# A hybrid diffusion block on one core: first token loads ahead of the first border, inverse transforms in the order of their inputs, VectorE combines in wider operations, precision splits after the third border

## The reference, cut to what matters

```python
def long_conv(u, kf, bias):
    length = u.shape[1]
    uf = jnp.fft.rfft(u, n=2 * length, axis=1)
    y = jnp.fft.irfft(uf * kf[None], n=2 * length, axis=1)[:, :length]
    return y + u * bias.astype(jnp.float32)

def hyena_branch(z, rows, conv_w, conv_b, filt, hy_bias):
    length = z.shape[1]
    z = short_conv_rows(z, rows, conv_w, conv_b).astype(jnp.float32)
    v, x1, x2 = jnp.split(z, 3, axis=-1)
    kf = hyena_filter_spectra(length, *filt)
    y = x1 * long_conv(v, kf[:, 0], hy_bias[0])
    return x2 * long_conv(y, kf[:, 1], hy_bias[1])
...
        hc = modulate(rmsnorm(ctx, norm1_g[l]), csh1, csc1)
...
        h = modulate(rmsnorm(x, norm1_g[l]), sh1, sc1)
        z = h @ w_in[l]
        u = z[..., HY_COLS:].astype(jnp.float32)
        st_f, st_b = s5_states(u, *s5_par, init_f, init_b)
        y = jnp.concatenate([hyena_branch(z[..., :HY_COLS], rows, conv_w[l], conv_b[l], filt, hy_bias[l]),
                             s5_readout(u, st_f, st_b, *s5_out)], axis=-1)
        x = x + g1[:, None] * (y.astype(x.dtype) @ w_out[l])
```

## Time and profile before

| what | value |
|---|---|
| timed runs, median (lowest to highest) | 2510.84 us (2508.46 to 2514.4), 3 runs |
| profiled execution, its own time | 2506.11 us |
| its span | 2504.4 us |
| `prepare` to the first border | about 239 us |
| `mix` | 239.5 to 534 us |
| `long_convs` | 535 to 751 us |
| TensorE, VectorE, ScalarE, GpSimd busy | 93%, 77%, 53%, 14% of the span |

### The profile page before, as it was taken

How to read it: one execution, slowest core, us unless ns; L and a number is a source line. 1 busy time by engine, 2 the same in 40 slices (tenths; PEclk the granted TensorE clock), 3 DMA queues, 4 the chain that set the end, 5 groups by cost and what they waited for, 6 DMA issues and landing times.

```text
span 2504.4 us, 27973 instructions
## 1 busy us (share of the span) xinstructions
PE 2330.7 (93%) x10978; PEld 1775.9 (71%) x10978; DVE 1940.8 (77%) x1424; ACT 1317.3 (53%) x788; POOL 361.7 (14%) x190
## 2 busy tenths in 40 slices
PE   7887989999988947999999999999999999999997
PEld 2334877853445835888888888888888888888886
DVE  4765799837584467888888888888888888888887
ACT  2123422210023216777777677677677677677766
POOL 0543400000002000012012022022022021021011
PEclk9898999999999967999999999999999999999998
DMA  7657344454432255999999999999999999999997
GB/s 271 226 226 261 123 110 128 138 213 149 151 147 85 85 235 185 379 376 366 374 378 373 366 378 374 372 372 379 370 370 377 374 369 375 379 367 373 378 360 294
DMA packets 199344, 726.40 MB, mean 290 GB/s; under 512 B 14050, under 2 KB 60034, under 8 KB 180277
## 3 DMA queue, kind: packets, MB, share of 16 engines
q1 hardware_dynamic: 190878, 694.03, 73.5%
q0 software_dynamic: 5328, 21.50, 3.1%
q10 hardware_dynamic: 3080, 10.09, 1.1%
HBM read 678.40 MB, written 47.17 MB: 290 GB/s over the span
## 4 chain that ended last, share of the span: by engine, by line
PE 55%; DVE 3%; issue 3%; ACT 1%; DMA 0%; POOL 0%; DVEq 0%; ACTq 0%; PEldq 0%; POOLq 0%
PE psum L2143 14%; PE psum L2130 13%; PE psum L2131 13%; PE psum L2132 13%; DVE w_low L2226 3%; PE psum L2111 2%; ACT x_high L2166 1%; ACT w_high L2162 0%; DVE arena L2240 0%; DMA out<-arena 0%; DVE x_low L2230 0%; DVE arena L2286 0%; DVE arena L2282 0%; POOL out L2091 0%; DVEq L2280 0%
## 5 line engine op out<-in xcount | busy, mean ns | idle before, releaser
L2226 DVE TENSOR_TENSOR w_low<-w_raw,w_high 128x4096 fp32r<-128x4096 f32 (+2 forms) x288 | 1164.1, 4065 | 95.3 <-ACT w_high L2162 95.3
L2162 ACT ACTIVATE w_high<-w_raw 128x4096 fp32r<-128x4096 f32 (+2 forms) x288 | 964.1, 3348 | 467.2 <-PE psum L2132 260.5
L2130 PE MATMUL psum<-w_high,x_high 128*128 128x512 f32 (+1 forms) x1536 | 578.0, 376 | 20.0 <-DVE w_low L2226 17.5
L2131 PE MATMUL psum<-w_low,x_high 128*128 128x512 f32 (+1 forms) x1536 | 573.5, 373 | 0.0
L2132 PE MATMUL psum<-w_high,x_low 128*128 128x512 f32 (+1 forms) x1536 | 571.9, 372 | 0.0
L2130 PEld LDWEIGHTS psum<-w_high,x_high 128*128 128x128 f32 x1536 | 290.0, 189 | 80.9 <-DVE w_low L2226 25.1
L2132 PEld LDWEIGHTS psum<-w_high,x_low 128*128 128x128 f32 x1536 | 289.2, 188 | 52.1
L2131 PEld LDWEIGHTS psum<-w_low,x_high 128*128 128x128 f32 x1536 | 289.7, 189 | 49.7
L2143 PE MATMUL psum<-w_high,a_high 128*128 128x512 f32 x704 | 220.8, 395 | 0.0
L2078 POOL TENSOR_TENSOR arena<-arena 1x1 f32<-1x1 f32 x15 | 63.2, 4214 | 1089.1 <-DVE arena L2282 1089.1
L2143 PE MATMUL psum<-w_low,a_high 128*128 128x512 f32 x704 | 217.3, 390 | 0.0
(11 more groups left out here) (361 smaller groups left out, 2638.9 us busy)
## 6 DMA issues: line engine op xcount, KB each, us to landing
w_raw<-in_ex_w_down SPq DMA_DIRECT2D x80, 2048.0 KB, 9.3
w_raw<-in_ex_w_gate SPq DMA_DIRECT2D x64, 2048.0 KB, 9.9
w_raw<-in_ex_w_up SPq DMA_DIRECT2D x64, 2048.0 KB, 10.5
w_raw<-in_ex_w_gate SPq DMA_DIRECT2D x32, 1536.0 KB, 10.4
w_raw<-in_ex_w_up SPq DMA_DIRECT2D x32, 1536.0 KB, 7.3
arena<-in_mod_w SPq DMA_DIRECT2D x24, 1024.0 KB, 6.2
w_raw<-in_ex_w_down SPq DMA_DIRECT2D x16, 1024.0 KB, 8.2
scratch_spec<-arena SPq DMA_DIRECT2D x8, 1024.0 KB, 10.2
```

The lines of the kernel that those rows point to most:

```text
L2130: nc.tensor.matmul(o, xt_h[:, x], h[:, f], start=kk == 0, stop=False)
L2131: nc.tensor.matmul(o, xt_h[:, x], l[:, f], start=False, stop=False)
L2162: nc.scalar.activation(high[n % NHI][:, 0:w], raw[n % NS][:, 0:w], ACT.Copy).then_inc(hi_done, 1)
L2226: nc.vector.tensor_tensor(low[n % NS][:, 0:w], raw[n % NS][:, 0:w], high[n % NHI][:, 0:w].bitcast(F32), ALU.subtract).then_inc(lo_done, 1)
```

## The change

Four edits, in words:

1. **First border.** The loads of the first 5 token tiles and of the first weight chunk are issued by SP in `prepare`, after the last filter matrices and before the last two writes of spectra. Their slots lie in memory that `prepare` no longer uses, and `c_high` and `c_low` move to where the slots were. The waits for the writes go from the end of `prepare` into `mix`: ACT waits for the S5 tables ahead of its first `high_tile` and for the spectra ahead of `scaled(4)`; SP waits for the S5 tables where it reads them. POOL's wait stays.
2. **Inverse transforms.** All eight banks take output tiles. The order is kk 0 of tiles 0 to 3, kk 1 of tiles 0 to 3, kk 0 and 1 of tiles 4 to 7, and then kk 2 of all eight.
3. **Combines.** The same arithmetic in 8 operations of 1024 or 2048 elements a partition (12 where f is 1).
4. **Splits.** The row blocks' high parts (4 on ACT) and the low parts (3 and 4 on VectorE) move into `output_and_route`; TensorE waits for them after the 32 matmuls of the S5 gate. The 3 high parts of weights stay.

```diff
@@ prepare, SyncE
             dft(7)
+            sp.wait_ge(used, NU)
+            for n, xin_slot in enumerate(k.token_slots):
+                src = k.i["x"][0, (n - 2) * P:(n - 1) * P, :] if n >= 2 else k.i["ctx"][0, n * P:(n + 1) * P, :]
+                sp.dma_start(xin_slot, src).then_inc(k.tokens_got[n], 16)
+            c = FIRST_CHUNK
+            sp.dma_start(k.w_in_first, k.i["w_in"].rearrange("l (k p) n -> p (l k) n", p=P)[:, :, c * P:(c + 1) * P]).then_inc(k.first_weights, 16)
             spec_out(2)
             spec_out(3)
-            for s in range(2):
-                sp.wait_ge(sput[s], 64)
             sp.wait_ge(rowput, 128)
@@ prepare, ScalarE
             quarter(3)
-            act.wait_ge(put_in, 64)
-            act.wait_ge(put_lw, 64)
@@ mix, SyncE
-            tokens(0)
-            tokens(1)
-            weights(0)
-            tokens(2)
-            tokens(3)
             weights(1)
-            tokens(4)
             weights(2)
-            for n in range(5, NT):
+            for n in range(NX, NT):
                 tokens(n)
+            sp.wait_ge(k.tables_in, 64)
             in_tables(0)
@@ mix, ScalarE
             high_part(0)
+            act.wait_ge(k.tables_in, 64)
+            act.wait_ge(k.local_put, 64)
             high_tile(0)
             high_tile(1)
+            for s in range(2):
+                act.wait_ge(k.spec_put[s], 64)
             scaled(4)
@@ long_convs, TensorE
                 pe.wait_ge(read, 4 * order + 3)
-                pe.wait_ge(done, 4 * order + 2 + order)
+                pe.wait_ge(done, 4 * order + 2)
                 for n in range(4):
-                    backward(order, n, (order,))
+                    backward(order, n, (0,))
                 pe.wait_ge(done, 4 * order + 3)
                 for n in range(4):
-                    backward(order, n, (1 - order,))
-                pe.wait_ge(done, 4 * order + 4)
-                for n in range(4):
-                    backward(order, n, (2,)).then_inc(inv, 1)
+                    backward(order, n, (1,))
                 pe.wait_ge(ring[2], loads + 32)
                 pe.wait_ge(ring[3], loads + 32)
+                pe.wait_ge(read, 4 * order + 4)
                 for n in range(4, 8):
-                    pe.wait_ge(fin, 8 * order + n - 3)
-                    backward(order, n, (order, 1 - order, 2)).then_inc(inv, 1)
+                    backward(order, n, (0, 1))
+                pe.wait_ge(done, 4 * order + 4)
+                for n in range(8):
+                    backward(order, n, (2,)).then_inc(inv, 1)
@@ long_convs, VectorE, combine (the 12 operations with the spectrum become these 4)
+                tt(bars(y), bars(x), kre, ALU.mult)
+                link(tt(bars(x), bars(x), kim, ALU.mult))
+                tt(y[:, 0:4:3, :], y[:, 0:4:3, :], x[:, 1:3, :], ALU.add)
+                link(tt(y[:, 1:3, :], y[:, 1:3, :], x[:, 0:4:3, :], ALU.subtract))
@@ output_and_route, TensorE, after the S5 gate
             pe.wait_ge(wlo, 1)
+            pe.wait_ge(wlo_first, 3)
+            pe.wait_ge(xlo, 4)
```

More of the change, by code:

```diff
@@ L240, in prepare @@
     dgot = [k.sem(f"d_got{s}") for s in range(2)]
-    sput = [k.sem(f"d_put{s}") for s in range(2)]
     row_banks = (6, 0)
@@ L1514, in backward @@
                 par, tile = divmod(n, 4)
-                o = ps[:, bank(order, 0) + n % 4, :]
+                o = ps[:, bank(par) + tile, :]
                 e, h = divmod(tile, 2)
-                first = order
                 for kk in kks:
```

131 lines of the change are left out of this document (56 added, 75 removed).

## The result

| | before | changed |
|---|---|---|
| median of the timed runs | 2510.43 us (2508.46 to 2514.4, 4 runs) | 2477.09 us (2473.23 to 2477.85, 4 runs) |
| profiled execution, its span | 2506.11, 2504.4 | 2477.30, 2475.5 |

The ratio is 0.9862, with a 95% interval from 0.9845 to 0.9879. The forecast was 2481.3 for the median and 2476.6 for the profiled execution.

The account below looks back on a forecast made before the run. TensorE, busy 93%, was taken as the bound, with its standstills in the first 752 us as the target. Terms 8.8 + 8.7 + 9.8 + 2.2 = 29.5 us, so 2510.8 - 29.5 = 2481.3 us; range 2475 to 2489.

Parts of the forecast that it names:

- First border, 8.8 us: Start of `mix`: ACT scales the first tile 8.8 us earlier, and VectorE, which paces the front, passes all on.
- Rival E: Little changes: a wait deeper in `mix` meets the border's gain and one order keeps its wait; 2500 us, chance 0.05.
- What hides the moved waits: In `mix`: tables land 4 us before ACT needs them, spectra are waited for 2 us later still; no cost charged.
- rival A: First border: moved loads delay squares, POOL's table, the last table or `mix`'s tiles; 2 to 6 us, 2483 to 2487, chance 0.18.
- Inverse transforms, 8.7 and 9.8 us: Long convolutions: TensorE never waits inside an inverse, each takes 41.3 us; 8.7 us saved in the first order, 9.8 in the second.
- the tightest spot: Second forward of f 0: ring slot 0's reload lands at 632.2, TensorE wants it at 633.0; 0.8 us to spare.
- rival C: Ring slot 0's reload comes too late, TensorE waits 9 us and the clock falls again; 2493 us, chance 0.04.
- Combines, nothing on the path: Long convolutions: wide combines save VectorE 5 us an order, but TensorE has its results early already; worth nothing, only slack.
- rival D: Combines: wide operations with steps between runs go at the rate of scattered elements; 31 us slower, 2542, chance 0.03.
- Splits and third border, 2.2 us: Third border: one `gated` follows the last matmul instead of 3.5 us of splits; 2.2 us gained, moved splits cost nothing.
- The clock at the third border, taken as 0 with 2.2 at the other end: S5 gate's start: clock assumed to fall in the shorter pause too, so gain 0; 2.2 us if it does not.
- rival B: Clock stays up at the third border and comes back sooner in `mix`'s front; 2.2 us more, 2479, chance 0.10.

Follow-up runs that it names:

- early split: Changed kernel with the first weight chunk's high and low parts also made at the end of the first stage; 2475.25 us, ratio 0.9863.
- combines undone: Changed kernel with the combines back in operations of 512, the rest kept; 2480.07 us, ratio 0.9877.
- order alone: Kernel before with only the new order of the inverse transforms and the eight banks it needs; 2499.7 us, ratio 0.9955.
- combines alone: Kernel before with only the combines in operations of 1024 and 2048; 2501.13 us, ratio 0.997.
- splits alone: Kernel before with only the splits moved into the next stage; 2506.28 us, ratio 0.9982.
- waits and loads: Changed kernel with the waits back at the first stage's end, 2484.71 us; and, separately, with the six loads issued by `mix` again, 2483.17 us.

## Why it came out so, step by step

**First border, 8.8 us: right at the place it was read, 0.6 to 1.8 less by the end of `mix`.** The front went from 10.40 to 1.59 us, 8.8 exactly. The prediction went on that VectorE, which paces the front of `mix`, would pass all of it on. It passed on 7.0 in this pair of profiles. Over the five profiles with the edit and nothing more at the border, `mix` takes 293.8 to 295.0 us, over the six without any of it 302.1 to 303.7 (means 294.6 and 302.8), 8.2. The step that was off is "VectorE too, since it had no idle time in which a part could get lost": its instructions can get longer. The low part of the first weights took 1.22 us before, and the second one 2.94:

```profile
251.76 1.22 DVE L1299 TENSOR_TENSOR p_wlow<-p_wraw,p_whigh 128x1024 fp32r<-128x1024 f32 x1
...
258.00 2.94 DVE L1299 TENSOR_TENSOR p_wlow<-p_wraw,p_whigh 128x1024 fp32r<-128x1024 f32 x1
```

In the changed kernel they took 3.01 and 2.16 us:

```profile
244.00 3.01 DVE L1309 TENSOR_TENSOR p_wlow<-p_wraw,p_whigh 128x1024 fp32r<-128x1024 f32 x1
...
252.04 2.16 DVE L1309 TENSOR_TENSOR p_wlow<-p_wraw,p_whigh 128x1024 fp32r<-128x1024 f32 x1
```

So 1.8 us are lost at the first and 0.8 won back at the second, 1.0 in all. The distance from ScalarE's first scaling to VectorE's first copy of 128x512 says the same: 42.89 us before (243.44 to 286.33), 43.91 now (235.68 to 279.59); it is 42.9 in five of the six profiles without the edit and 43.7 to 44.0 in the five with it. The other 0.8 of this pair lies behind that copy, in a stretch that takes 247.6 to 250.5 us over the fourteen profiles; it is of the size of their scatter. For the first of the two operations GpSimd has a subtraction of its own, at 243.57, beside VectorE's of 244.00:

```profile
243.57 2.36 POOL L1287 TENSOR_TENSOR p_clow<-p_h,p_chigh 128x1024 fp32r<-128x1024 f32 x1 [19.54 <-ACT p_chigh L1182]
```

In the six profiles in which GpSimd's came first, by 0.2 to 0.6 us, VectorE's took 2.84 to 3.23 us; in the seven in which it came 0.5 to 1.0 us behind, VectorE's took 1.21 to 1.23. That GpSimd's work is the cause was not tested by itself; the early split takes this operation out of `mix`, and its `mix` is 1.5 us shorter. Rival E, a wait deeper in `mix`, did not come.

**What hides the moved waits: right, and rival A's collisions cost nothing on the path.** Neither the tables nor the spectra were waited for in `mix`. The queue's length did show, where the prediction had looked: GpSimd's last table took 9.9 us to land, by the view of DMA issues from 200 to 240 us of the changed kernel, instead of the 4.2 of the earlier trace rows, and GpSimd came to the border at 233.4 instead of 226.6, still 1.1 us ahead of ScalarE's 234.5. ScalarE's loads for the means took 7.4 us in the median of four (6.1 before), and two squares waited for them, 2.27 and 0.91 us. The mean was not later for it: from VectorE's 128x10 operation to the issue of `s_local` are 4.09 us in both profiles. The transfers:

```profile
scratch_s_out<-arena POOLq DMA_DIRECT2D x1, 1024.0 KB, 9.9
...
arena<-in_x ACTq DMA_DIRECT2D x4, 512.0 KB, 7.4
```

By the Trainium skill ("DMA: Bandwidth & Descriptors", "Queues, rings and completion order") a DMA engine takes turns between the queues that have work, a packet at a time. By that rule a queue beside a full one becomes slower and doesn't stand behind it. The rows agree, the 9.9 us as well: from 215 to 230 us, around that write, the windows give the DMA engines a busy share of 0.56 before and 1.03 now. The prediction's reading, that it costs nil, holds for a moment at which the queue was full already; at GpSimd's write it had not been.

**Inverse transforms, 8.7 and 9.8 us: right, 8.8 and 9.6 measured.** Forward to inverse to forward, TensorE's timeline of the changed kernel:

```profile
529.10 57.37 PE L1520 MATMUL psum<-arena 128*128 128x512 f32 x128 [1.62 <-PEq L181]
586.31 41.36 PE L1534 MATMUL psum<-arena 128*128 128x512 f32 x96
627.51 55.10 PE L1520 MATMUL psum<-arena 128*128 128x512 f32 x128
682.44 7.07 PE L1538 MATMUL psum<-arena 128*128 128x256 f32 x32
```

The first inverse took 41.2 us, the second 41.45 (682.44 to 723.89), at a clock of 1.00. The saving was 8.8 and 9.6. The reload of ring slot 0, "the tightest spot", came in time (rival C out).

**Combines, nothing on the path: right for the inverses in this order, and only there.** With the new order, plain combines leave the convolutions at 194.7 and 195.7 us against 194.8. But a term was missing behind them: with the new order and combines of 512 the norm row comes too late at the third border, and in combines undone the pause is 0.7 us longer and the gate 1.7. With the old order the same edit is worth 9.5 (203.3 against 212.8). So the 18.5 us are not the order's alone: the order alone brings 18.1, the combines alone 9.5, both together 18.0, because they cure one wait. Read from the changed kernel, undoing the order costs 9.8 us, half of what the prediction's terms say, and that is no contradiction. On VectorE they cost what was forecast: 11.70 us for a plain one (578.98 to 590.68) and 18.76 for f 1 (forecast 11.7 and 18.7), and no operation pays for its strides or its repeated operand (rival D out):

```profile
551.02 2.28 DVE L1612 TENSOR_TENSOR arena<-arena 128x2048 f32<-128x2048 f32 x1
553.34 1.23 DVE L1613 TENSOR_TENSOR arena<-arena 128x1024 f32<-128x1024 f32 x1
554.49 1.22 DVE L1614 TENSOR_TENSOR arena<-arena 128x1024 f32<-128x1024 f32 x1
...
578.98 1.22 DVE L1605 TENSOR_TENSOR arena<-psum,arena 128x1024 f32<-128x1024 f32 x1
...
590.68 1.22 DVE L1605 TENSOR_TENSOR arena<-psum,arena 128x1024 f32<-128x1024 f32 x1
```

An order needs 56 instructions fewer. VectorE saved 4.9 us (58.72 to 53.86), 0.09 us for each; by the 157 ns of the Trainium skill ("VectorE: DVE Perf Modes", "The TRN2 errata") it would be 8.8. The spacing of the rows was the right price.

**Splits and third border, 2.2 us: the sum right, the share wrong.** The pause went from 4.40 to 2.01 us, and no split was waited for at the gate's end:

```profile
725.90 5.69 DVE L1827 TENSOR_TENSOR g_wlow<-arena,g_whigh 128x1024 fp32r<-128x1024 f32 x3 [0.86 <-PEq L181]
731.51 4.62 DVE L1830 TENSOR_TENSOR g_xlow<-arena,g_xhigh 128x1024 fp32r<-128x1024 f32 x4
```

But the prediction set the moved splits against the border of before, and never asked what the new order does to that border. It lengthens the pause by 4.3 to 5.9 us when the splits stay (8.69 and 10.34). With the new order, the splits' edit is worth 6.7 us of pause, and 2.9 more at the gate; without it, 2.4 and 0.5.

**The clock at the third border, taken as 0 with 2.2 at the other end: the other end came.** The gate took 27.70 us instead of 29.92, at a granted clock of 1.00 from its start. This is rival B's gain at this border. It belongs to no single edit: without the wide combines the gate took 29.40 us although the splits were moved (splits alone, combines undone). The profiled executions then add up: 7.0 in mix, 18.0 in the convolutions (8.8 and 9.6, and 0.2 in the second forward, less 0.6 in the first, where the clock fell at another place), 2.4 and 2.2 make 29.7; less 1.05 by which the first stage came out longer, and with 0.3 behind the gate, it is the 28.9 us between the spans.

**The step from profile to median: what is left open.** The medians differ by 33.3 us, the profiled executions by 28.8. The kernel before was profiled in an execution faster than all four timed ones of the result; the changed kernel's profile fell on its median. Over the 14 profiles `s_local` is issued from 230.9 to 243.4 us. That does not go with the border's edit (mean 236.4 with the loads in the first stage and 237.7 without) but with TensorE's granted clock in the first stage. Its mean from 50 to 200 us is 0.97 in the profile with 230.9; 0.92 to 0.93 in the four with 232.1 to 234.1; 0.90 to 0.91 in the four with 235.5 to 237.4; and 0.87 to 0.89 in the five with 241.4 to 243.4. What sets that clock in an execution is not shown. Such scatter covers the 4.5 us, but no run shows that it is all of it. The single medians add up no better: alone the four edits give 7.1, 11.2, 8.0 and 2.9 us, 29.2 together, and the total is 33.3. That the forecast of the median, 2481.3, came within 4.2 us is in part such scatter; by the profiled executions the 29.5 us of the sum met 28.8, and there the gate's 2.2 us, taken as 0, made up for what was short in `mix`.

## What to carry to other kernels

When a change has several edits, cost each against the kernel in which the others are already made, in both directions: one edit can do what another does (order and combines), one can create the cost that another removes (order and splits), and two can be worth more together than the sum of each alone (waits and loads, by the profiles). When outputs are moved to the end of a stage, read what stands between and behind them in the queue of the engine that stores them: work that fitted between tiles 5 us apart becomes a tail behind tiles 1.7 us apart. When executions differ by 10 us in a part that the change leaves alone, compare distances between marks in the profiles, and take the medians for the sum only. Know the scatter of such a distance as well, from several kernels that leave it alone, before a microsecond of it is given to an edit.

## What the runs showed of the hardware

- **The clock at the gate.** In all seven profiles with a pause of 2.01 us the gate took 27.70 us, full clock throughout. After pauses of 4.39 and 4.40 it took 29.92 to 29.95, after 8.69 and 10.34 it took 30.56 and 29.10. But after 2.02 us in splits alone and 2.69 in combines undone it took 29.40, so the pause alone does not decide it. Those two have the moved splits with combines of 512; the seven have the moved splits with wide ones. How the combines would bear on it was not tested.
- **VectorE's strides.** An operation of 128x2048 with a repeated operand, or one of 1024 over every second bank of PSUM, costs what its element count says: the next one starts 2.20 and 1.14 us later, 0.11 more behind a semaphore.
- **A write beside a filled queue.** GpSimd's 1 MB took 9.9 us instead of 4.2 (8.8 to 9.9 in the seven profiles with the loads in the first stage, 4.2 to 4.5 in the seven without).
- **VectorE beside GpSimd.** The same 128x1024 subtraction took 1.21 to 1.23 us when GpSimd's own began 0.5 to 1.0 us behind it (seven profiles) and 2.84 to 3.23 us when GpSimd's began 0.2 to 0.6 us ahead of it (six).
- **The length of the first stage.** It varies by 12 us between executions, together with the mean granted clock from 50 to 200 us, 0.97 at the shortest and 0.87 at the longest.
